# A fast-product feed-forward whose scaled operand blocks are made in another order between two stages

## The chip, the cores and the metric

The kernel runs on one core of one Trainium2 chip. The metric is the device time of one execution in microseconds (us); three executions of the kernel before gave a median of 2181.12 us. All tensors are float32. "ScalarE" is the engine ACT of the profile, "VectorE" is DVE, "GpSimd" is POOL, "TensorE" is PE.

## The reference

Two layers over a prompt of 512 tokens and 8 sample tokens (520 columns in all), width 1024:

```
x = x + 1/2 * SwiGLU_a(RMSNorm(x))
x = x + Mixer_m(RMSNorm(x))      # layer 0: gated MLP with chunked spatial mixing, layer 1: latent attention
x = x + 1/2 * SwiGLU_b(RMSNorm(x))

def swiglu(h, w_gate, w_up, w_down):
    return (silu(h @ w_gate) * (h @ w_up)) @ w_down
def rms_norm(x, g):
    return x * rsqrt(mean(x * x) + EPS) * g
```

The hidden width of a SwiGLU is 2816. There are four of them (0 to 3 here), each with its own gain and weights.

## The kernel before

**Data.** `x` is held transposed: 8 tiles of 128 channels by 520 columns. Every product is done in split precision: an operand is cut into a high part (`_hi`, a copy rounded by ScalarE) and a rest (`_lo`, value minus high part, by VectorE), and TensorE does three matmuls, high by high, rest by high, high by rest.

**Gate and up products.** In most of each SwiGLU they are done by a seven-product scheme on 2 x 2 blocks (tile pair by column half of 260). For a pair i of x tiles (2i, 2i+1) there are seven operand blocks `xw_hi[:, i, j, :]`, `xw_lo[:, i, j, :]`, j = 0 to 6. With a, b the low and high columns of the even tile and c, d those of the odd tile, all times the gain: block 0 is a, block 1 is a - b, blocks 3 and 5 are c and d, and blocks 2, 4 and 6 are differences of these, built by VectorE as `blocks[:, 2:5, :]`. `blocks[:, 0, :]` holds the gained b for this. The weights have seven block sums too (`sums_w`). A "chunk" is seven such products of 12 matmuls each (three for each of the four pairs, k = 0 to 3). Product j = 2 adds onto the PSUM bank of product 0, so ScalarE must first copy product 0 aside (L1281, `snapped`).

**The hand-over.** At the end of the stage before (gMLP output for SwiGLU 1, SwiGLU 1's last down product for SwiGLU 2, attention output for SwiGLU 3) TensorE makes eight tiles in four pairs ("down", 48 matmuls a tile). VectorE updates x (L1734, or L1874 and L1877), and in the same loop the norm operands are made: ScalarE `fast_norm` (L1307: high parts), VectorE `fast_norm` (L1839: differences and rests), ScalarE squares x and GpSimd adds the squares up (L2403), for the sum over channels that TensorE takes with a matrix of ones (`rms`, L686). ScalarE turns it into a root (L1330), VectorE into a reciprocal (L1715), which scales the products' results when they leave PSUM; so products may begin before the sum is known. In the last pair VectorE also prepares the first weight chunk (`fast_first`, L1774).

SwiGLU 0 builds the same blocks once at the start, beside products of another form, with `first_blocks` in place of `blocks`.

**Order.** There is no scheduler: each engine runs its own list in the order written, and waits on semaphores. `xg_hi_done` counts ScalarE's high parts, `xg_lo_done` VectorE's rests, `block_set` the differences, `evac_done` updates of x and evacuations of PSUM, `lo_done` weight rests. The counts at each stage's start are in class `At`.

## Time and profile before

| what | value |
|---|---|
| median of 3 runs | 2181.12 us (2179.63 to 2183.32) |
| the profiled execution, its own time | 2180.65 us |
| its span | 2178.9 us |
| PE busy | 2118.2 us, 97% |
| DVE busy | 1526.7 us, 70% |
| ACT busy | 994.8 us, 46% |
| POOL busy | 207.7 us, 10% |
| mean granted clock | 0.991 |

The profile is of one execution. Times in its rows count from the start of the span. A row of a timeline has start, duration, engine, source line, instruction, output <- inputs, partitions x elements, and in brackets the engine's idle time before it with what ended that. Consecutive instructions of VectorE and ScalarE overlap by about 0.1 us in their records.

### The profile page before, as it was taken

To read this page: it belongs to the slowest core of one execution; us is meant where nothing else is said; L and a number is where in the kernel's file an instruction comes from. 1 tells how busy PE (TensorE), PEld (TensorE's weight loads), DVE (VectorE), ACT (ScalarE), POOL (GpSimd) and SP (SyncE) were. 2 spreads that over 40 slices of the span, in tenths; PEclk is the share of its full clock that TensorE was granted. 3 is DMA by queue.
4 is the path that set the end of the run, shared out by engine and by line. 5 is a ranking of instruction groups with operands and counts; after the bars stand their busy time and mean duration, and the time that the engine had idled before them with its cause. 6 is when DMAs were issued, how large, how long until landed. Compare 5 with 4: busy or idle time off the path is not lost.

```text
span 2178.9 us, 42803 instructions
## 1 busy us (share of the span) xinstructions
PE 2118.2 (97%) x17012; PEld 2042.3 (94%) x17012; DVE 1526.7 (70%) x2222; ACT 994.8 (46%) x1549; POOL 207.7 (10%) x199
## 2 busy tenths in 40 slices
PE   8999999999998999999799999999999998999999
PEld 8999999999998999999799999987668788999999
DVE  7787685335358878597878769577665469787683
ACT  6445363433235535254444536344554445454352
POOL 0100001124031000000000000123121120000000
PEclk9999999999999999999899999999999999999999
DMA  6233233232221323232132322341221112323232
GB/s 182 78 97 116 78 98 114 80 95 74 83 79 59 102 92 116 82 112 97 59 111 92 126 78 96 116 116 36 82 88 59 59 40 78 105 89 122 74 116 76
DMA packets 203635, 198.85 MB, mean 91 GB/s; under 512 B 12071, under 2 KB 200788, under 8 KB 203252
## 3 DMA queue, kind: packets, MB, share of 16 engines
q1 hardware_dynamic: 202938, 196.67, 28.3%
q8 instruction: 86, 1.41, 0.3%
q10 hardware_dynamic: 314, 0.37, 0.1%
q14 instruction: 41, 0.34, 0.1%
q0 software_dynamic: 256, 0.07, 0.0%
HBM read 194.42 MB, written 2.66 MB: 90 GB/s over the span
## 4 chain that ended last, share of the span: by engine, by line
PE 85%; DVE 8%; ACT 3%; issue 2%; POOL 1%; DMA 0%; SPq 0%; DVEq 0%; ACTq 0%; POOLq 0%
PE main L676 35%; PE side L725 21%; PE main L725 16%; PE side L1221 2%; PE main L993 1%; DVE blocks L1859 1%; PE side L1188 1%; DVE w_lo L1710 1%; PE main L1151 1%; PE side L1024 1%; ACT w_hi L1251 1%; DVE w_lo L1737 1%; PE side L1077 1%; PE main L1056 1%; PE side L912 1%
## 5 line engine op out<-in xcount | busy, mean ns | idle before, releaser
L725 PE MATMUL side<-xw_hi,w_hi 128*128 128x260 f32 x1344 | 383.9, 286 | 25.3 <-ACT main L1281 18.0
L676 PE MATMUL main<-h_hi,w_hi 128*128 128x260 f32 x1920 | 387.5, 283 | 4.0 <-DVE x L1877 2.3
L676 PE MATMUL main<-h_hi,w_lo 128*128 128x260 f32 x1920 | 387.1, 283 | 0.0
L676 PE MATMUL main<-h_lo,w_hi 128*128 128x260 f32 x1920 | 386.4, 283 | 0.0
L725 PE MATMUL side<-xw_hi,w_lo 128*128 128x260 f32 x1344 | 381.6, 284 | 0.0
L725 PE MATMUL side<-xw_lo,w_hi 128*128 128x260 f32 x1344 | 380.2, 283 | 0.0
L676 PEld LDWEIGHTS main<-h_hi,w_hi 128*128 128x128 f32 x1920 | 296.3, 189 | 4.9 <-issue 2.7
L676 PEld LDWEIGHTS main<-h_hi,w_lo 128*128 128x128 f32 x1920 | 296.4, 189 | 0.0
L676 PEld LDWEIGHTS main<-h_lo,w_hi 128*128 128x128 f32 x1920 | 295.6, 189 | 0.0
L725 PE MATMUL main<-xw_hi,w_hi 128*128 128x260 f32 x1008 | 288.9, 287 | 2.3 <-DVE tmp_mul L1942 2.3
L725 PE MATMUL main<-xw_lo,w_hi 128*128 128x260 f32 x1008 | 288.4, 286 | 0.0
L725 PE MATMUL main<-xw_hi,w_lo 128*128 128x260 f32 x1008 | 287.9, 286 | 0.0
L725 PEld LDWEIGHTS side<-xw_hi,w_hi 128*128 128x128 f32 x1344 | 255.1, 190 | 27.5 <-ACT main L1281 19.3
L725 PEld LDWEIGHTS side<-xw_hi,w_lo 128*128 128x128 f32 x1344 | 255.1, 190 | 0.0
L725 PEld LDWEIGHTS side<-xw_lo,w_hi 128*128 128x128 f32 x1344 | 254.7, 190 | 0.1
L1710 DVE TENSOR_TENSOR w_lo<-raw,w_hi 128x2048 fp32r<-128x2048 f32 x70 | 160.5, 2293 | 108.6 <-ACT w_hi L1251 105.1
L1737 DVE TENSOR_TENSOR w_lo<-raw,w_hi 128x512 fp32r<-128x512 f32 (+1 forms) x276 | 202.6, 734 | 24.2 <-ACT w_hi L1290 13.5
L1251 ACT ACTIVATE w_hi<-raw 128x2048 fp32r<-128x2048 f32 x66 | 125.8, 1906 | 177.4 <-PE main L676 177.4
L1737 DVE TENSOR_TENSOR w_lo<-sums_w,w_hi 128x1024 fp32r<-128x1024 f32 x168 | 205.0, 1220 | 1.7 <-ACT w_hi L1273 1.6
L725 PEld LDWEIGHTS main<-xw_hi,w_hi 128*128 128x128 f32 x1008 | 192.9, 191 | 2.5 <-DVE w_lo L1737 2.5
L725 PEld LDWEIGHTS main<-xw_lo,w_hi 128*128 128x128 f32 x1008 | 192.8, 191 | 0.0
L725 PEld LDWEIGHTS main<-xw_hi,w_lo 128*128 128x128 f32 x1008 | 192.5, 191 | 0.0
(385 smaller groups left out, 3645.0 us busy)
## 6 DMA issues: line engine op xcount, KB each, us to landing
raw<-in_ffn_w_up SPq DMA_DIRECT2D x44, 1024.0 KB, 5.1
raw<-in_ffn_w_gate SPq DMA_DIRECT2D x43, 1024.0 KB, 5.1
raw<-in_ffn_w_down SPq DMA_DIRECT2D x32, 1024.0 KB, 5.2
raw<-in_gmlp_w_in SPq DMA_DIRECT2D x16, 1024.0 KB, 5.4
raw<-in_ffn_w_down SPq DMA_DIRECT2D x16, 768.0 KB, 4.4
raw<-in_gmlp_w_out SPq DMA_DIRECT2D x8, 1024.0 KB, 5.2
raw<-in_mla_w_o SPq DMA_DIRECT2D x8, 1024.0 KB, 5.5
over<-in_cache_mla SPq DMA_DIRECT2D x64, 104.0 KB, 1.9
```

The lines of the kernel that those rows point to most:

```text
L676: mm = nc.tensor.matmul(into[:, half, 0:HALF], w[:, k, m * P:(m + 1) * P], moving[:, k, half * HALF:(half + 1) * HALF], start=(k == 0 and ...
L725: mm = nc.tensor.matmul(into[j], w_tiles(w, j)[:, k, :], moving[:, k, j, :], start=(j in (0, 1) and k == 0 and i == 0), stop=(k == 3 and i ...
L912: mm = nc.tensor.matmul(side[:, bank, q * P:(q + 1) * P], v_tok[:, m, q, :], ws_t[:, g, :], start=True, stop=True)
L993: mm = nc.tensor.matmul(main[:, u % 2, half, 0:HALF], st, moving[:, k, half * HALF:(half + 1) * HALF], start=(k == 0 and i == 0), stop=(k ...
L1024: nc.tensor.matmul(side[0:w, i % 2, :], c_t[:, b * P:b * P + w], wkv[:, 4 * j:4 * j + 4, :].rearrange("p h n -> p (h n)"), start=True, sto ...
L1056: mm = nc.tensor.matmul(main[:, h % 2, half, 0:HALF], wuk_t[:, h % 2, :], qn[:, h, half * HALF:(half + 1) * HALF], start=True, stop=True)
L1077: t_ = nc.tensor.transpose(side[:, bank, i * P:(i + 1) * P], pieces[2 * (first + i // 2) + half][:, j0 + i % 2, c0:c0 + P], ident)
L1151: nc.tensor.matmul(main[:, q // 2, q % 2, 0:nk], q_rope[lo:lo + ROPE, :], kr_t[lo:lo + ROPE, 0:nk], start=False, stop=True).then_inc(score ...
L1221: mm = nc.tensor.matmul(side[:, 2, k * P:SEQ], rows[:, k, 0:KL], prob_t[:, PT_AT[k] * P:(PT_AT[k] + QB - k) * P], start=(k == 0), stop=(k ...
L1251: nc.scalar.activation(w_hi[:, 1 - s, :], raw[:, 1 - s, :], ACT.Copy).then_inc(hi_done, 1)
L1710: nc.vector.tensor_tensor(w_lo[:, 1 - s, :], raw[:, 1 - s, :], w_hi[:, 1 - s, :].bitcast(F32), ALU.subtract).then_inc(lo_done, 1)
L1737: a = nc.vector.tensor_tensor(dst, src, hi.bitcast(F32), ALU.subtract)
```

## The change

1. ScalarE's copy of the gained high columns into `blocks[:, 0, :]` moves from the odd tile's part to the even tile's part of each pair, and it signals `xg_hi_done`. So a pair has five high-part signals (six in the last), and a new counter `xh` keeps them; `xg` goes on counting rests. VectorE's first difference waits for this copy alone, and its rest of blocks 3 and 5 waits for the high parts of the odd tile.
2. In the last pair, ScalarE takes the weight step `fast_third` ahead of the odd tile's update, makes only blocks 3 and 5 there (`last_hi`), and goes on to the first chunk: copy of product 0, then high part of block 2, of blocks 4 and 6 (`last_blocks_hi`), copy of product 1, squares of tile 7, and then the weight block that stood between.
3. VectorE's `fast_first` is cut in two: two weight rests move behind the even tile's part of the last pair. In the odd part the rest of block 2 comes first, then blocks 3 and 5, then a weight rest (`rest_sums(4, 0)`), then blocks 4 and 6; the last rests are two instructions where there was one.
4. TensorE waits for the rests one product at a time (2: count 15, 3: 16, 4: 17), and takes the sum of squares ahead of product 5 instead of product 4.

```diff
-                                    x_waits = {(0, 0): x + 12, (0, 3): x + 13, (1, 3): x + 14, (2, 3): x + 16}
-                                    between = {4: rms(at, 2)}
+                                    x_waits = {(0, 0): x + 12, (0, 3): x + 13, (1, 3): x + 14, (2, 3): x + 15, (3, 3): x + 16,
+                                               (4, 3): x + 17}
+                                    between = {5: rms(at, 2)}
...
-                nc.scalar.activation(w_tiles(w_hi, 6), raw_parts(s)[:, 3], ACT.Copy).then_inc(hi_done, 1)
+                if tail:
+                    tail[0]()
+                else:
+                    nc.scalar.activation(w_tiles(w_hi, 6), raw_parts(s)[:, 3], ACT.Copy).then_inc(hi_done, 1)
                 act.wait_ge(tile_done, t + 2)
                 act.wait_ge(evac_done, e - 2)
                 nc.scalar.activation(snap[:, 0, :], main[:, 0, 0, 0:HALF], ACT.Copy, scale=-1.0).then_inc(snapped, 1)
+                if tail:
+                    tail[1]()
+                    nc.scalar.activation(w_tiles(w_hi, 6), raw_parts(s)[:, 3], ACT.Copy).then_inc(hi_done, 1)
...
                     nc.scalar.activation(xw_hi[:, i, 1, :], blocks[:, 1, :], ACT.Copy, scale=g0).then_inc(xg_hi_done, 1)
+                    nc.scalar.activation(blocks[:, 0, :], x[:, 2 * i, HALF:TOK], ACT.Copy, scale=g0).then_inc(xg_hi_done, 1)
                 elif part == 1:
-                    nc.scalar.activation(blocks[:, 0, :], x[:, 2 * i, HALF:TOK], ACT.Copy, scale=g0)
...
+            def last_hi(norm):
+
+                nc.scalar.activation(xw_hi[:, 3, 3:6:2, :], x_halves(KD - 1), ACT.Copy,
+                                     scale=gain[:, norm, KD - 1:KD]).then_inc(xg_hi_done, 1)
+
+            def last_blocks_hi(b):
+
+                act.wait_ge(block_set, b + 2)
+                nc.scalar.activation(xw_hi[:, 3, 2, :], blocks[:, 2, :], ACT.Copy).then_inc(xg_hi_done, 1)
+                act.wait_ge(block_set, b + 3)
+                nc.scalar.activation(xw_hi[:, 3, 4:7:2, :], blocks[:, 3:5, :], ACT.Copy).then_inc(xg_hi_done, 1)
...
                         if fast:
+                            if k == KD - 1:
+                                fast_third(at.tile, at.wsum)
                             act.wait_ge(evac_done, e + k + 1)
+                            if k == KD - 1:
+                                last_hi(at.norm)
+                                continue
...
+                    if between:
+                        dve.wait_ge(xg_hi_done, hi + 3)
+                        take_rest(xw_lo[:, i, 2, :], blocks[:, 2, :], xw_hi[:, i, 2, :], xg_lo_done)
+                    dve.wait_ge(xg_hi_done, hi + 2)
                     nc.vector.scalar_tensor_tensor(xw_lo[:, i, 3:6:2, :], x_halves(2 * i + 1), gains[1],
                                                    xw_hi[:, i, 3:6:2, :].bitcast(F32), ALU.mult, ALU.subtract).then_inc(xg_lo_done, 1)
                     dve.wait_ge(block_set, b + 3)
-                    dve.wait_ge(xg_hi_done, hi + 2)
-                    take_rest(xw_lo[:, i, 2:7:2, :], blocks[:, 2:5, :], xw_hi[:, i, 2:7:2, :], xg_lo_done)
+                    if between:
+                        between()
+                        dve.wait_ge(xg_hi_done, hi + 4)
+                        take_rest(xw_lo[:, i, 4:7:2, :], blocks[:, 3:5, :], xw_hi[:, i, 4:7:2, :], xg_lo_done)
+                    else:
+                        dve.wait_ge(xg_hi_done, hi + 3)
+                        take_rest(xw_lo[:, i, 2:7:2, :], blocks[:, 2:5, :], xw_hi[:, i, 2:7:2, :], xg_lo_done)
```

ScalarE in one of the pairs before the last, at the hand-over to SwiGLU 1; `blocks` is the scratch of differences, `square` the squares that GpSimd adds. Before:

```order
L1311 ACTIVATE xw_hi<-x,vectors 128x260 [waits evac_done]
L1313 ACTIVATE xw_hi<-blocks,vectors 128x260 [waits block_set]
L1257 ACTIVATE square<-x 128x520 [waits sum_done]
L1315 ACTIVATE blocks<-x,vectors 128x260 [waits evac_done]
L1316 ACTIVATE xw_hi<-x,vectors 128x2x260
L1257 ACTIVATE square<-x 128x520 [waits sum_done]
L1319 ACTIVATE xw_hi<-blocks 128x3x260 [waits block_set]
```

The same pair in the changed kernel:

```order
L1319 ACTIVATE xw_hi<-x,vectors 128x260 [waits evac_done]
L1321 ACTIVATE xw_hi<-blocks,vectors 128x260 [waits block_set]
L1322 ACTIVATE blocks<-x,vectors 128x260
L1259 ACTIVATE square<-x 128x520 [waits sum_done]
L1324 ACTIVATE xw_hi<-x,vectors 128x2x260 [waits evac_done]
L1259 ACTIVATE square<-x 128x520 [waits sum_done]
L1327 ACTIVATE xw_hi<-blocks 128x3x260 [waits block_set]
```

The copy into `blocks` stands ahead of the even tile's squares, and no longer behind the odd tile's update.

ScalarE in the last pair and the start of the first chunk; `main<-side` is the copy of product 0, `snap<-main` that of product 1. Before:

```order
L1313 ACTIVATE xw_hi<-blocks,vectors 128x260 [waits block_set]
L1257 ACTIVATE square<-x 128x520 [waits sum_done]
L1315 ACTIVATE blocks<-x,vectors 128x260 [waits evac_done]
L1316 ACTIVATE xw_hi<-x,vectors 128x2x260
L1257 ACTIVATE square<-x 128x520 [waits sum_done]
L1319 ACTIVATE xw_hi<-blocks 128x3x260 [waits block_set]
L1273 ACTIVATE w_hi<-sums_w 128x1024 [waits weights_summed,tile_done]
L1281 ACTIVATE main<-side 128x260 [waits evac_done,tile_done]
L1282 ACTIVATE w_hi<-raw 128x512
L1285 ACTIVATE snap<-main 128x260 [waits evac_done,tile_done]
```

In the changed kernel:

```order
L1321 ACTIVATE xw_hi<-blocks,vectors 128x260 [waits block_set]
L1322 ACTIVATE blocks<-x,vectors 128x260
L1259 ACTIVATE square<-x 128x520 [waits sum_done]
L1275 ACTIVATE w_hi<-sums_w 128x1024 [waits weights_summed,tile_done]
L1331 ACTIVATE xw_hi<-x,vectors 128x2x260 [waits evac_done]
L1283 ACTIVATE main<-side 128x260 [waits evac_done,tile_done]
L1337 ACTIVATE xw_hi<-blocks 128x260 [waits block_set]
L1339 ACTIVATE xw_hi<-blocks 128x2x260 [waits block_set]
L1290 ACTIVATE snap<-main 128x260 [waits evac_done,tile_done]
L1259 ACTIVATE square<-x 128x520 [waits sum_done]
L1293 ACTIVATE w_hi<-raw 128x512
```

The copy of product 0 now has one 2 x 260 instruction between it and the update of tile 7 (`evac_done`), and the last squares come six instructions after that update.

VectorE in the last pair, `w_lo` being weight rests and `x<-main,x` the updates of tiles 6 and 7. Before:

```order
L1737 TENSOR_TENSOR w_lo<-sums_w,w_hi 128x1024 [waits hi_done]
L1737 TENSOR_TENSOR w_lo<-raw,w_hi 128x512 [waits hi_done]
L1734 SCALAR_TENSOR_TENSOR x<-main,x 128x520 [waits tile_done]
L1845 TENSOR_TENSOR blocks<-x 128x260 [waits evac_done]
L1848 SCALAR_TENSOR_TENSOR xw_lo<-x,vectors,xw_hi 128x260 [waits xg_hi_done]
L1852 SCALAR_TENSOR_TENSOR xw_lo<-blocks,vectors,xw_hi 128x260 [waits xg_hi_done,block_set]
L1734 SCALAR_TENSOR_TENSOR x<-main,x 128x520 [waits tile_done]
L1856 SCALAR_TENSOR_TENSOR blocks<-x,vectors,blocks 128x260 [waits xg_hi_done,evac_done]
L1859 SCALAR_TENSOR_TENSOR blocks<-x,gain_neg,blocks 128x260 [waits block_set]
L1862 SCALAR_TENSOR_TENSOR blocks<-x,gain_neg,blocks 128x260 [waits block_set]
L1864 SCALAR_TENSOR_TENSOR xw_lo<-x,vectors,xw_hi 128x2x260
L1737 TENSOR_TENSOR xw_lo<-blocks,xw_hi 128x3x260 [waits xg_hi_done,block_set]
```

In the changed kernel (the update of tile 6 stands ahead of the first row):

```order
L1882 SCALAR_TENSOR_TENSOR xw_lo<-blocks,vectors,xw_hi 128x260 [waits xg_hi_done,block_set]
L1765 TENSOR_TENSOR w_lo<-sums_w,w_hi 128x1024 [waits hi_done]
L1765 TENSOR_TENSOR w_lo<-raw,w_hi 128x512 [waits hi_done]
L1762 SCALAR_TENSOR_TENSOR x<-main,x 128x520 [waits tile_done]
L1886 SCALAR_TENSOR_TENSOR blocks<-x,vectors,blocks 128x260 [waits xg_hi_done,evac_done]
L1889 SCALAR_TENSOR_TENSOR blocks<-x,gain_neg,blocks 128x260 [waits block_set]
L1892 SCALAR_TENSOR_TENSOR blocks<-x,gain_neg,blocks 128x260 [waits block_set]
L1765 TENSOR_TENSOR xw_lo<-blocks,xw_hi 128x260 [waits xg_hi_done]
L1898 SCALAR_TENSOR_TENSOR xw_lo<-x,vectors,xw_hi 128x2x260 [waits xg_hi_done]
L1765 TENSOR_TENSOR w_lo<-sums_w,w_hi 128x1024 [waits hi_done,block_set]
L1765 TENSOR_TENSOR xw_lo<-blocks,xw_hi 128x2x260 [waits xg_hi_done]
```

Two weight rests moved from ahead of the update of tile 6 to ahead of that of tile 7, and the update of tile 7 has the same instructions ahead of it as before.

## Rows read from the trace of the kernel before

**Rows 1.** The page, part 4: engines' shares of the chain that ended last.
```profile
PE 85%; DVE 8%; ACT 3%; issue 2%; POOL 1%; DMA 0%; SPq 0%; DVEq 0%; ACTq 0%; POOLq 0%
```

**Rows 2.** Waits of PE: us in total, times, longest us.
```profile
PE side L725 <- ACT main L1281: 18.0, 6, 5.4
...
PE main L725 <- DVE tmp_mul L1942: 2.3, 1, 2.3
PE main L676 <- DVE x L1877: 2.3, 2, 2.0
```

**Rows 3.** Timeline of PE, hand-overs to SwiGLU 1 and 3.
```profile
694.97 0.58 PE L725 MATMUL side<-xw_hi,w_hi 128*128 128x260 f32 x1 [5.02 <-ACT main L1281]
...
710.29 0.39 PE L725 MATMUL side<-xw_hi,w_hi 128*128 128x260 f32 x1 [2.05 <-ACT main L1281]
...
1814.85 0.39 PE L725 MATMUL side<-xw_hi,w_hi 128*128 128x260 f32 x1 [3.15 <-DVE x L1734]
```

**Rows 4.** Timeline of VectorE, last pair and first chunk, hand-over to SwiGLU 1.
```profile
686.05 0.69 DVE L1734 SCALAR_TENSOR_TENSOR x<-main,x 128x520 f32<-128x520 f32 x1
...
688.25 0.69 DVE L1734 SCALAR_TENSOR_TENSOR x<-main,x 128x520 f32<-128x520 f32 x1
690.22 0.49 DVE L1856 SCALAR_TENSOR_TENSOR blocks<-x,vectors,blocks 128x260 f32<-128x260 f32 x1 [1.27 <-ACT xw_hi L1316]
690.74 1.54 DVE L1859 SCALAR_TENSOR_TENSOR blocks<-x,gain_neg,blocks 128x260 f32<-128x260 f32 x1
...
693.80 0.97 DVE L1737 TENSOR_TENSOR xw_lo<-blocks,xw_hi 128x780 fp32r<-128x780 f32 x1 [0.32 <-ACT xw_hi L1319]
...
704.30 3.39 DVE L1715 RECIPROCAL rstd_all<-root 128x520 f32<-128x520 f32 x1
```

**Rows 5.** Timeline of ScalarE, same place.
```profile
692.84 0.85 ACT L1319 ACTIVATE xw_hi<-blocks 128x780 fp32r<-128x780 f32 x1 [2.20 <-DVE blocks L1862]
...
694.55 0.37 ACT L1281 ACTIVATE main<-side 128x260 f32<-128x260 f32 x1
```

**Rows 6.** Timeline of GpSimd, same place.
```profile
688.35 1.32 POOL L2403 TENSOR_TENSOR square_sum<-square_sum,square 128x520 f32<-128x520 f32 x1 [9.82 <-ACT square L1257]
690.72 1.28 POOL L2403 TENSOR_TENSOR square_sum<-square_sum,square 128x520 f32<-128x520 f32 x1 [1.05 <-ACT square L1257]
```

**Rows 7.** Line L1859, all its instructions: ns min/median/max, first and last start us.
```profile
L1859 DVE SCALAR_TENSOR_TENSOR blocks<-x,gain_neg,blocks x12: 1540/1570/1589, 653.8 to 1816.6; 128x260 f32<-128x260 f32 x12
L1859 DVE SCALAR_TENSOR_TENSOR sums_w<-x,gain_neg,sums_w x4: 487/490/490, 35.2 to 58.6; 128x260 f32<-128x260 f32 x4
```

**Rows 8.** Timeline of GpSimd in SwiGLU 0.
```profile
65.80 2.98 POOL L2408 TENSOR_TENSOR h_lo<-tmp_h,h_hi 128x520 fp32r<-128x520 f32 x2 [42.18 <-ACT h_hi L1393]
```

**Rows 9.** Timeline of VectorE in SwiGLU 0.
```profile
34.66 0.49 DVE L1856 SCALAR_TENSOR_TENSOR sums_w<-x,vectors,sums_w 128x260 f32<-128x260 f32 x1 [0.47 <-ACT xw_hi L1316]
...
65.84 1.78 DVE L1737 TENSOR_TENSOR w_lo<-raw,w_hi 128x512 fp32r<-128x512 f32 x1
```

**Rows 10.** Timeline of VectorE, first chunk of SwiGLU 3.
```profile
1821.88 1.22 DVE L1747 TENSOR_TENSOR sums_w<-raw 128x1024 f32<-128x1024 f32 x1
...
1828.17 3.39 DVE L1715 RECIPROCAL rstd_all<-root 128x520 f32<-128x520 f32 x1
```

**Rows 11.** Timeline of VectorE, hand-over to SwiGLU 2.
```profile
1019.71 2.30 DVE L1710 TENSOR_TENSOR w_lo<-raw,w_hi 128x2048 fp32r<-128x2048 f32 x1 [0.77 <-ACT w_hi L1251]
...
1033.45 2.29 DVE L1710 TENSOR_TENSOR w_lo<-raw,w_hi 128x2048 fp32r<-128x2048 f32 x1 [0.77 <-ACT w_hi L1251]
...
1054.81 1.23 DVE L1877 SCALAR_TENSOR_TENSOR x<-tmp_mul,x 128x520 f32<-128x520 f32 x1
...
1072.11 3.39 DVE L1715 RECIPROCAL rstd_all<-root 128x520 f32<-128x520 f32 x1
```

**Rows 12.** The chain that ended last, a pair of down tiles: start us, us, what.
```profile
1765.58 11.53 PE main L676 x96
```

**Rows 13.** Busy time by stretch: us, PE, PEld, DVE, ACT, POOL busy, granted clock, DMA share, GB/s.
```profile
695.00:700.00 5.00, 5.00 (x25) 5.00 (x25) 4.54 (x6) 2.70 (x5) 0.00 (x0) 0.54 0.10 31
```

More of the change, by code:

```diff
@@ L84 @@
     FIELDS = ("chunk", "extra", "tile", "evac", "h", "mul", "act", "norm", "rms", "sums", "snap", "wsum", "rows",
-              "xg", "blocks")
+              "xg", "xh", "blocks")
     def __init__(self, **counts):
         (self.chunk, self.extra, self.tile, self.evac, self.h, self.mul, self.act, self.norm, self.rms, self.sums, self.snap,
-         self.wsum, self.rows, self.xg, self.blocks) = (counts.get(f, 0) for f in self.FIELDS)
+         self.wsum, self.rows, self.xg, self.xh, self.blocks) = (counts.get(f, 0) for f in self.FIELDS)
         self.lo = self.chunk + self.extra
     def past(self, chunk=0, extra=0, tile=0, evac=0, h=0, mul=0, act=0, norm=0, rms=0, sums=0, snap=0, wsum=0, rows=0,
-             xg=0, blocks=0):
+             xg=0, xh=0, blocks=0):
         return At(chunk=self.chunk + chunk, extra=self.extra + extra, tile=self.tile + tile, evac=self.evac + evac,
@@ L96, in past @@
                   sums=self.sums + sums, snap=self.snap + snap, wsum=self.wsum + wsum, rows=self.rows + rows,
-                  xg=self.xg + xg, blocks=self.blocks + blocks)
+                  xg=self.xg + xg, xh=self.xh + xh, blocks=self.blocks + blocks)
 def ffn_past(at, plain=0, last=False):
@@ L104, in ffn_past @@
                    evac=8 * fast + 4 * plain + 8 * groups, h=2 * pairs, act=2 * pairs, norm=1, rms=1, sums=0 if last else KD,
-                   snap=6 * fast, wsum=6 * fast, rows=2 * fast + 8 * groups, xg=16 + KD * (plain > 0), blocks=16)
+                   snap=6 * fast, wsum=6 * fast, rows=2 * fast + 8 * groups, xg=16 + KD if plain else 17,
+                   xh=20 + KD if plain else 21, blocks=16)
 def bc(ap, n):
@@ L442, in program @@
         at_ffn[1] = at_gmlp.past(chunk=gmlp_chunks, tile=2 * gmlp_chunks, evac=2 * gmlp_chunks, h=GT, mul=GT, act=2 * GT, norm=1,
-                                  rms=2, sums=GT + KD, xg=KD)
+                                  rms=2, sums=GT + KD, xg=KD, xh=KD)
         at_ffn[2] = ffn_past(at_ffn[1])
@@ L447, in program @@
         at_wo = at_uq.past(chunk=4, tile=24, evac=24)
-        at_ffn[3] = at_wo.past(chunk=8, tile=16, evac=16, h=H, norm=1, sums=KD, xg=KD)
+        at_ffn[3] = at_wo.past(chunk=8, tile=16, evac=16, h=H, norm=1, sums=KD, xg=KD, xh=KD)
         P_AT = [0, 1, 3, 6]
@@ L1274, in fast_third, with fast_chunk @@
                                      ACT.Copy).then_inc(hi_done, 1)
-            def fast_chunk(s, raw_ready, t, e, w, after, middle=None):
+            def fast_chunk(s, raw_ready, t, e, w, after, middle=None, tail=None):
                 act.wait_ge(tile_done, t + 1)
@@ L1357, in gate_up @@
                         fast_chunk(0, 16 * (n // 2 + i + 1), t + 14 * i, e + 8 * i, w + 6 * i, "fast",
-                                   (lambda: rms_root(at, 2)) if first else None)
+                                   (lambda: rms_root(at, 2)) if first else None,
+                                   (lambda: last_blocks_hi(at.blocks + 13),
+                                    lambda: squares(x[:, KD - 1:KD, :], 1, at.sums - 1)) if first else None)
                         for m in range(2):
@@ L1397, in ffn @@
                     else:
-                        fast_third(t, w)
+                        if g > 0:
+                            fast_third(t, w)
                         if g == 0:
@@ L1772, in rest_sums, with fast_first @@
                 take_rest(w_block(w_lo, j, 2), sums_w[:, at:at + 2, :].rearrange("p a c -> p (a c)"), w_block(w_hi, j, 2), lo_done)
-            def fast_first(s, raw_ready, l, w):
-                sums_outer(s, raw_ready)
-                sums_second(s, w)
-                rest_raw(s, 0, 0, l + 1)
-                sums_last(s, w)
-                rest_sums(1, 2, l + 2)
-                rest_raw(s, 3, 2, l + 3)
+            def fast_first(s, raw_ready, l, w, parts=(0, 1)):
+                if 0 in parts:
+                    sums_outer(s, raw_ready)
+                    sums_second(s, w)
+                    rest_raw(s, 0, 0, l + 1)
+                    sums_last(s, w)
+                if 1 in parts:
+                    rest_sums(1, 2, l + 2)
+                    rest_raw(s, 3, 2, l + 3)
             def fast_chunk(s, raw_ready, t, e, l, w, sn, into, by, after, ready=None, late=None):
@@ L1837, in h_rest, with fast_norm @@
                                         ALU.subtract).then_inc(h_lo_done, n)
-            def fast_norm(norm, i, part, b, hi, blocks=blocks):
+            def fast_norm(norm, i, part, b, hi, blocks=blocks, between=None):
                 gains = [gain[:, norm, 2 * i + m:2 * i + m + 1] for m in range(2)]
@@ L1935, in norm_pair @@
                             for part in range(2):
-                                fast_norm(0, i, part, 4 * i + part, KD + 4 * i + 2 * part, first_blocks)
+                                fast_norm(0, i, part, 4 * i + part, KD + 5 * i + 2 * part, first_blocks)
                         def plain_up(i, m, dst):
```

12 lines of the change are left out of this document (8 added, 4 removed).

## The prediction

> **What bounds the kernel now.** I read the chain of waits first: TensorE is 85% of it, VectorE 8%, ScalarE 3% [rows 1]. So nearly all the time is matmul work that this change leaves alone, and what can be won is where the chain leaves TensorE. The waits of PE say where: 18.0 us in six waits of seven-product matmuls for ScalarE's L1281, the copy of product 0 aside [rows 2]. The timeline splits them: at each hand-over to SwiGLU 1, 2 and 3 there is one before product 2 and one before product 2 of the second half of the chunk, as 5.02 and 2.05 us at the first; at the third TensorE waits 3.15 us for the update of x before product 0 [rows 3]. ScalarE is not short of time there. L1281 is late because it stands behind L1319, which waited 2.20 us for VectorE's differences [rows 5]. VectorE in turn waited 1.27 us for ScalarE and 0.32 us for it again, and one difference took 1.54 us [rows 4]. The same line takes 0.49 us in SwiGLU 0 [rows 7], where GpSimd adds no squares. At the hand-over GpSimd's add started at 690.72, 0.02 us ahead of the long difference, for 1.28 us [rows 4, 6]. I read it as a lock: while GpSimd runs an add, a VectorE instruction with two SBUF inputs waits. It goes both ways: a weight rest that began with a GpSimd pair at 65.8 took 1.78 us, and the pair 2.98 us where two adds of 1.3 us would take 2.6 [rows 6, 8, 9]. The update of x, which reads PSUM, ran at 688.25 in its usual 0.69 us beside an add [rows 4, 6]. So VectorE's list is the bound of a hand-over, with 1.3 us to pay where an add meets it.
>
> **The second wait.** The reciprocal starts at 704.30 and TensorE goes on at 710.29, 5.99 us later [rows 3, 4]. Nothing in that stretch is changed. So each hand-over is worth what the start of its reciprocal moves.
>
> I call T the end of the update of tile 7, and split at it. Before, T is 688.94 (688.25 + 0.69), 1056.04 (1054.81 + 1.23) and 1814.80 (0.05 us ahead of the matmul that it releases), and the reciprocals start at 704.30, 1072.11 and 1828.17: 15.36, 16.07 and 13.37 us after T [rows 3, 4, 10, 11].
>
> **Behind T, the new order.** VectorE then has three differences (0.53 us from start to start, the 0.49 with its gap), the rest of block 2 (half as long as the others, about 0.4), the rest of blocks 3 and 5 (0.7), the weight rest (1.15) and the rest of blocks 4 and 6 (0.65): 4.4 us by the durations of rows 4 and 7 and by width. The copy of b is made early, so the 1.27 us are gone. The long difference is short, since the add of tile 6's squares is over by then. But the last squares are now the sixth of ScalarE's instructions behind T; they end about 3.0 us after T, GpSimd's add is ready during the weight rest and takes 1.3 us when that ends, and the rest of blocks 4 and 6 waits for it. Then come the sums and evacuations of the first chunk, whose start to reciprocal is 6.29 us where VectorE has no gap, as in SwiGLU 3 [rows 10]. In the other two it had gaps there, since the products came late. Sum: 4.4 + 1.3 + 6.3 = 12.0 us. That is 3.4 us off at the first hand-over and 4.1 at the second. At the third TensorE starts product 0 only at T, so L1281 can't run before about T + 1.7, and the high part of block 2 stands behind it: VectorE idles some 0.9 us, 12.9 us in all, 0.5 off.
>
> What is added there: one more VectorE and one or two more ScalarE instructions, counted above. TensorE will wait less before product 2 (L1281 now ends 0.7 us behind T), but again before product 6, for an evacuation that VectorE does about 1 us ahead of the reciprocal, while product 5 ends some 8 us after T: a new wait of 2 to 3 us, which the sum by the reciprocal contains. The later sum of squares is hidden: it is ready about 5 us after T, root and table load before T + 11.7. That is close: without VectorE's backlog it would be next.
>
> **Ahead of T.** In each earlier pair VectorE's idle 1.27 us goes. What is given back: the even squares are one instruction (about 0.4 us) later, so their add, which started 1.61 us after the update of tile 6 (686.74 to 688.35) [rows 4, 6] and lay beside the odd update, starts at 2.0 us and meets the first difference, up to 1.1 us, wherever VectorE runs without waiting for TensorE. Where the odd update waits for its tile, that add is past. The odd add moves from the second difference to the rest of blocks 3 and 5, same price, but the high parts and the weight copy of ScalarE (0.32 and 0.77 us of waits) now fit in beside it: 1.27 + 0.32 + 0.77, up to 2.4 us a pair [rows 4, 11].
> - SwiGLU 2: updates are two instructions, and VectorE's period is 13.74 us a pair (1019.71 to 1033.45) against TensorE's 11.53 [rows 11, 12]. Here every saved microsecond counts: 2.3 in the first pair, about 1.5 more in each of the next two (tile by tile against TensorE), 5.3 at the end of the third; less 1.3 for the add on the moved weight rest, plus 0.5 since tile 7's update, 1.23 us beside an add [rows 11], is 0.70 free of it: 4.5, of which I take 4.4. The waits of TensorE for L1877, 2.3 us [rows 2], go with it.
> - SwiGLU 1: without the second instruction of the updates (two of 0.73 us and the 0.53 of the add on one) the period is 11.75, 0.2 above TensorE's. So the third pair's odd update can move only 0.4, that pair's end 1.6 more; 1.3 comes back in the last pair, and T moves 0.6. Its bounds are 0 and 2.0.
> - SwiGLU 3: like 1, T moves 0.6.
>
> **SwiGLU 0.** The first difference waited 0.47 us for L1316 [rows 9]; it now waits for the copy one instruction ahead. Four pairs make 1.8 us. VectorE has no slack there: TensorE waited 2.3 us for L1942 behind these blocks [rows 2]. Bounds 0.5 (one pair) and 1.8; I take 1.8.
>
> **Sum.** SwiGLU 0: 1.8; 1: 0.6 + 3.4 = 4.0; 2: 4.4 + 4.1 = 8.5; 3: 0.6 + 0.5 = 1.1. Together 15.4 us. The profiled execution took 2180.65 us, so 2165.2; the median lies 0.5 us above it: 2165.7, say 2166.
>
> The cost that no row shows is who goes first when an add and a two-input instruction meet in the new places. I charge 1.3 us in full at five kinds of place. Its lower bound is 0 (row 688.35: an add beside an update costs nothing), its upper 1.1 to 1.3 each (1.54 or 1.78 us for 0.49 and 0.68).
>
> The Trainium skill, page "GPSIMD Engine Reference", section Key points, says that GpSimd shares its SBUF interfaces with VectorE, contending with instructions that have two SBUF inputs. By it the rests and weight sums that I move beside the adds must pay like the difference of rows 7, and the first rival below can't be; no row here shows an add beside a 260-column rest.
>
> **Rivals.**
> - *A, the adds cost nothing in their new places.* For: the add at 688.35 ran beside an update for nothing [rows 4, 6]. Against: the stretched instructions [rows 7 to 9]. Without them, T moves 1.7 us more in 1 and 3 and 2.4 in 2, and 1.3 more behind each T: 9.7 more, 2156.
> - *B, only the part behind T comes.* The adds on the first differences (1.1 us in each of three pairs) eat what the early copy gives, and the adds on the weight rest the remainder. For: in a pair where VectorE never waits, the first difference would start 3.4 us after the even update in both orders. Left: 3.4 + 4.1 + 0.5 and about 0.5 of SwiGLU 0: 8.5 us, 2172.5.
> - *C, it moves the wait and no more.* ScalarE's chain takes over: copy, high parts and squares in a row put the root behind VectorE's backlog, or the copies that TensorE needs before products 4 and 6 wait for more. T + 12 becomes T + 14 at the first two hand-overs, and nothing at the third: 1.4 + 2.1, 3.5 us off, 2177.5.
> - *D, slower: the clock.* After the 5.02 us wait TensorE ran at a granted 0.54 of its clock for 5 us [rows 13], the lower of its levels of 1.2 and 2.4 GHz, at half the pace. The new order has four waits of 0.8 to 3 us within 20 us. If the clock stays low for more than about 10 us per hand-over after the reciprocal, when TensorE is the bound again, 5 us each or 15 in all, the gain is gone; at 14 us each the time is 2187. Against it: the matmul behind the 2.05 us wait at 710.29 took 0.39 us, at full clock, where the one at 694.97 took 0.58 [rows 3], and no wait of the new order is as long as 5 us.
>
> The Trainium skill, page "TensorE: Matmul & The Clock Gate", Part 1, has the array fall to half rate when idle; by it the fewer long waits speak for full clock, and D asks for many short ones to count as idle.
>
> **How the numbers follow.** Forecast 0.52, A 0.12, B 0.20, C 0.10, D 0.06. The forecast's own range is 2162 to 2170 (SwiGLU 0's bounds and one add per hand-over either way). For 8 in 10 I go to 2156 and 2176, which leaves out C, D and a part of A. A measurement here can tell about 0.2%, 4.4 us, from no change: the forecast, A and B are faster by more, C half of the time no change, and D is slower in most. Faster 0.87, same 0.09, slower 0.04.
>
> **What would show it.** The reciprocals start 12 us after the update of tile 7 (13 in SwiGLU 3); PE's wait for L1281 before product 2 at the first hand-over falls from 5.0 to about 1 us, the one after the reciprocal stays at 2 to 3, and a new one for an evacuation stands before product 6. Differences take 0.49 us in the last pair, and some rest or weight instruction 1.1 to 1.3 us more, beside an add. In SwiGLU 2 the down tiles run without a wait for L1877's successor. I am wrong if the differences still take 1.5 us and VectorE idles behind T, or if TensorE's granted clock is near 0.5 for longer than 5 us behind a reciprocal.

## The result, and the profile after

| | before | after |
|---|---|---|
| median | 2180.48 us (2179.63 to 2183.32, 4 runs) | 2165.56 us (2162.85 to 2166.58, 4 runs) |
| profiled execution, its span | 2180.65, 2178.9 us | 2166.24, 2164.5 us |
| mean granted clock | 0.991 | 0.994 |

The ratio is 0.9929, with an interval of 0.9917 to 0.9941: 13 to 18 us off, where 2166.0 us was forecast. The page of the kernel after, part 4, shares of the chain that ended last, answers to [rows 1]:

```profile
PE 90%; DVE 5%; issue 2%; ACT 1%; POOL 1%; DMA 0%; SPq 0%; DVEq 0%; POOLq 0%; ACTq 0%
```

VectorE and ScalarE together have lost 5 of their 11 points. Waits of PE (us in total, times, longest), which answer to [rows 2]:

```profile
PE side L726 <- ACT main L1283: 8.3, 6, 2.4
PE side L726 <- DVE tmp_in L1841: 7.8, 4, 2.5
...
PE side L726 <- DVE x L1762: 2.2, 1, 2.2
```

The waits for the copy of product 0 (L1283, L1281 before) fall from 18.0 to 8.3 us. The waits for the down tiles' update (L1877) and for L1942 are gone. The 7.8 us for the evacuation L1841, before product 6, are 5.3 us at the three hand-overs, which are new, and 2.5 us in SwiGLU 0, where TensorE had waited 1.1 us for the same evacuation (L1811 in the kernel before):

```profile
PE side L725 <- DVE tmp_in L1811: 1.1, 1, 1.1
```

VectorE at the hand-over to SwiGLU 1, from the moved weight rest on, answers to [rows 4]:

```profile
684.20 1.80 DVE L1765 TENSOR_TENSOR w_lo<-raw,w_hi 128x512 fp32r<-128x512 f32 x1
685.92 0.69 DVE L1762 SCALAR_TENSOR_TENSOR x<-main,x 128x520 f32<-128x520 f32 x1
686.64 0.49 DVE L1886 SCALAR_TENSOR_TENSOR blocks<-x,vectors,blocks 128x260 f32<-128x260 f32 x1
687.17 0.49 DVE L1889 SCALAR_TENSOR_TENSOR blocks<-x,gain_neg,blocks 128x260 f32<-128x260 f32 x1
...
690.30 1.80 DVE L1765 TENSOR_TENSOR xw_lo<-blocks,xw_hi 128x520 fp32r<-128x520 f32 x1
...
698.31 3.38 DVE L1743 RECIPROCAL rstd_all<-root 128x520 f32<-128x520 f32 x1
```

VectorE has no idle time left here, the differences are short, and two rests take 1.80 us where they would take 0.68. The timeline of GpSimd there answers to [rows 6]:

```profile
683.56 1.88 POOL L2446 TENSOR_TENSOR square_sum<-square_sum,square 128x520 f32<-128x520 f32 x1 [7.13 <-ACT square L1259]
689.74 1.80 POOL L2446 TENSOR_TENSOR square_sum<-square_sum,square 128x520 f32<-128x520 f32 x1 [4.29 <-ACT square L1259]
```

Each add started while the instruction ahead of a long rest still ran, took 1.80 to 1.88 us instead of 1.3, and the rest after that instruction was long. TensorE's waits there answer to [rows 3]:

```profile
687.70 0.39 PE L726 MATMUL side<-xw_hi,w_hi 128*128 128x260 f32 x1 [0.35 <-ACT main L1283]
691.12 0.36 PE L726 MATMUL side<-xw_hi,w_hi 128*128 128x260 f32 x1 [0.26 <-ACT snap L1301]
697.59 0.36 PE L726 MATMUL side<-xw_hi,w_hi 128*128 128x260 f32 x1 [2.48 <-DVE tmp_in L1841]
704.30 0.39 PE L726 MATMUL side<-xw_hi,w_hi 128*128 128x260 f32 x1 [0.62 <-ACT main L1283]
```

The wait of 5.02 us before product 2 is 0.35 us, and the last row starts 5.99 us after the reciprocal, as before.

**One table for all kernels.** A hand-over is measured from the start of tile 0's update (in SwiGLU 2 the second of its two instructions) to T, and from T to the start of the reciprocal ("tail"), in each profiled execution. What lies outside is SwiGLU 0, and code that no kernel here changes. "Short adds" are explained below, under "The lock". Each run was compared with runs of the kernel before on its own chip (medians 2180.3 to 2181.6 us); the ratios below are of those.

| kernel | median us | to SwiGLU 1: to T + tail | to SwiGLU 2 | to SwiGLU 3 | sum |
|---|---|---|---|---|---|
| before | 2180.48 | 43.04 + 15.36 | 49.44 + 16.07 | 43.43 + 13.37 | 180.7 |
| new order, old wait | 2180.48 | 44.16 + 12.93 | 49.99 + 12.93 | 44.53 + 13.96 | 178.5 |
| signal alone | 2168.93 | 41.57 + 13.17 | 44.99 + 13.56 | 41.97 + 12.34 | 167.6 |
| early copy, old order | 2166.66 | 40.95 + 14.45 | 44.33 + 12.54 | 41.36 + 14.47 | 168.1 |
| new order and signal | 2170.31 | 42.70 + 12.31 | 45.54 + 12.31 | 43.06 + 13.12 | 169.0 |
| after | 2165.56 | 42.05 + 11.70 | 44.50 + 11.70 | 42.43 + 13.41 | 165.8 |
| before, short adds | 2171.03 | 41.54 + 13.79 | 44.58 + 14.69 | 41.95 + 13.78 | 170.3 |
| after, short adds | 2159.88 | 40.67 + 10.69 | 42.17 + 10.61 | 41.06 + 11.58 | 156.8 |
| after, rests back | 2164.09 | 40.95 + 12.59 | 44.37 + 11.70 | 41.36 + 12.70 | 163.7 |
| after, last square to TensorE | 2163.82 | 42.05 + 10.59 | 44.50 + 10.77 | 42.44 + 12.61 | 163.0 |
| after, no wait at SwiGLU 3 | 2164.55 | 42.07 + 11.70 | 44.53 + 11.69 | 42.47 + 11.70 | 164.2 |
| those three together | 2162.15 | 40.94 + 11.48 | 44.35 + 10.60 | 41.37 + 11.47 | 160.2 |
| two squares to TensorE, no wait | 2160.30 | 40.94 + 10.65 | 43.41 + 10.65 | 41.34 + 10.65 | 157.6 |

The hand-overs lose 14.9 us (180.7 to 165.8). SwiGLU 0, from its first rest (33.24, now 32.56) to its first down tile (89.93, now 87.04), loses 2.2 more. That is 17.1 us where the span lost 14.4: 3.4 us were lost in code that did not change, and 0.7 won before the first rest. Of the 3.4, 1.5 are between SwiGLU 0 and the first hand-over, where the kernel after has a half-clock piece (granted clock 0.57 from 476.5 to 480.5) and the kernel before has none. Another 1.8 are between the second and the third hand-over, in the attention, where TensorE fell to half clock for a while in this execution. The same place before (first row) and after (second), with the granted clock as third number from the right:

```profile
1596.00:1618.00 22.00, 18.73 (x107) 12.50 (x104) 15.41 (x47) 13.26 (x30) 7.37 (x6) 1.00 0.22 73
```
```profile
1579.00:1602.00 23.00, 19.76 (x98) 13.49 (x95) 13.67 (x39) 12.12 (x27) 7.44 (x6) 0.85 0.21 69
```

The stretch from the second reciprocal to the third hand-over took 698.0 to 702.1 us in the 13 profiles, with such half-clock pieces at different places, and all that lies outside the hand-overs (SwiGLU 0 with it) took 1996.2 to 2003.7 us. So one profile's end tells a kernel's gain only to several us, while the same steps in two kernels agree in the table to some 0.05 us (the kernel after and the one without the wait at SwiGLU 3: 42.05 and 42.07, 44.50 and 44.53).

The medians show less than these sums. In the kernel after, the hand-overs and SwiGLU 0 won 17.1 us and the median 14.9; with short adds on it, 26.1 and 20.7; with two squares to TensorE, 24.0 and 20.0. I did not follow where the remainder goes in each kernel: the table tells where time is won, and the medians how much of it the whole kernel shows.

### The profile page after: what moved, and what is told of

Read it like the earlier page. It is cut to its first block, busy times and chain, and to the rows that moved or that the text cites. A ratio compares the mean times of both kernels' runs of the same rounds, so it can differ in the third digit from the quotient of the medians.

```text
span 2164.5 us, 42809 instructions
## 1 busy us (share of the span) xinstructions
PE 2115.6 (98%) x17012; PEld 2039.2 (94%) x17012; DVE 1526.8 (71%) x2225; ACT 995.0 (46%) x1552; POOL 212.1 (10%) x199
## 4 chain that ended last, share of the span: by engine, by line
PE 90%; DVE 5%; issue 2%; ACT 1%; POOL 1%; DMA 0%; SPq 0%; DVEq 0%; POOLq 0%; ACTq 0%
PE main L677 40%; PE side L726 21%; PE main L726 16%; PE side L1223 2%; PE main L995 1%; PE side L1190 1%; DVE w_lo L1765 1%; PE main L1153 1%; PE side L1026 1%; PE side L1079 1%; PE main L1058 1%; PE side L914 1%; PE main L1140 1%; DVE rstd_all L1743 0%; PE main L1142 0%
## 5 line engine op out<-in xcount | busy, mean ns | idle before, releaser
L1765 DVE TENSOR_TENSOR w_lo<-raw,w_hi 128x512 fp32r<-128x512 f32 (+1 forms) x276 | 204.8, 742 | 24.2 <-ACT w_hi L1298 13.5
```

What stands on the lines that cost most here:

```text
L1765: a = nc.vector.tensor_tensor(dst, src, hi.bitcast(F32), ALU.subtract)
```

## Experiments

**The three edits of the change taken apart.** First the early, signalling copy alone, on the kernel before:

```diff
                     nc.scalar.activation(xw_hi[:, i, 1, :], blocks[:, 1, :], ...).then_inc(xg_hi_done, 1)
+                    nc.scalar.activation(blocks[:, 0, :], x[:, 2 * i, HALF:TOK], ...).then_inc(xg_hi_done, 1)
                 elif part == 1:
-                    nc.scalar.activation(blocks[:, 0, :], x[:, 2 * i, HALF:TOK], ...)
```

> The kernel before with one edit alone: ScalarE makes the scaled copy of b with the even tile and signals it, VectorE's first difference waits for that; the last pair and the first chunk keep their old order. Theory (VectorE's list is the bound, the order behind T is worth its own part): VectorE's idle 1.27 us go in every pair. SwiGLU 0 about 1 us, SwiGLU 1 and 3 0.6 us each ahead of T and 1.3 us behind T at the first two hand-overs, SwiGLU 2 about 4.4 us ahead of T: 9 to 10 us in all, 2171 us; a difference or the rest of blocks 3 and 5 still takes 1.5 to 1.8 us behind T, beside the add of tile 6's squares. Rival (the adds that come one ScalarE instruction later eat what the copy gives): under 3 us, 2178 us or more, and the whole gain is in the new order of the last pair.

2166.66 us, ratio 0.994 (0.9928 to 0.9953): 13.9 us off where 9 to 10 were expected. Its tail at the hand-over to SwiGLU 1 is 14.45 us, since now both adds meet differences:

```profile
686.06 1.36 DVE L1877 SCALAR_TENSOR_TENSOR blocks<-x,vectors,blocks 128x260 f32<-128x260 f32 x1
687.46 1.51 DVE L1880 SCALAR_TENSOR_TENSOR blocks<-x,gain_neg,blocks 128x260 f32<-128x260 f32 x1
```

Then the new order with b copied late again, but signalled (the last pair likewise):

```diff
-                    nc.scalar.activation(blocks[:, 0, :], ...).then_inc(xg_hi_done, 1)
                 elif part == 1:
+                    nc.scalar.activation(blocks[:, 0, :], ...).then_inc(xg_hi_done, 1)
```

> The kernel after with the early copy undone: b is copied with the odd tile again, signalled, and VectorE's first difference waits for it; the last pair and the first chunk keep their new order. Theory: the wait of 1.27 us is back in every pair, T stands where it stood before but for the weight rest (up to 1.3 us later), and behind T the reciprocal comes 2 to 3 us earlier than before at the first two hand-overs: 4 to 6 us off the kernel before, 2175 us. Rival (the early copy gives nothing): as the kernel after, 2166 us.

2170.31 us, ratio 0.9953 (0.994 to 0.9966): 5 us faster than I expected "the order" to be. The trace showed why this was no clean undoing: the first difference waits 0.65 us, not 1.27. Before, it waited for ScalarE's instruction behind the copy; the signal frees it at the copy. So I took the signal away too:

```diff
                 else:
-                    dve.wait_ge(xg_hi_done, hi + 1)
+                    dve.wait_ge(xg_hi_done, hi + 2)
                     nc.vector.scalar_tensor_tensor(blocks[:, 3, :], ...
```

> The new order of the last pair and the first chunk, and nothing else: b is copied with the odd tile, and the first difference waits, as in the kernel before, for ScalarE's next instruction behind that copy too (the high part of blocks 3 and 5). The run with the copy alone signalled waited 0.65 us there in place of 1.27. Theory: the signal is worth 0.6 us in every pair: behind each T, in three pairs of SwiGLU 2 and in SwiGLU 0's four: 5 to 6 us slower than that run, 2175 to 2176 us, which leaves 5 us for the order alone. Rival: the adds fall on other instructions and eat the difference, 2171 us.

2180.48 us, ratio 1.0 (0.9991 to 1.0009, 11 runs): the order alone is worth nothing that the median can show, though the hand-overs take 2.2 us less. Both numbers of mine were too low. What it wins in the tails (2.4 and 3.1 us) it loses in part ahead of T (1.1, 0.6 and 1.1 us, the add on the moved weight rest) and at SwiGLU 3. And at the other end of the ladder, the signal with nothing else:

```diff
-                    nc.scalar.activation(blocks[:, 0, :], x[:, 2 * i, HALF:TOK], ACT.Copy, scale=g0)
+                    nc.scalar.activation(blocks[:, 0, :], x[:, 2 * i, HALF:TOK], ACT.Copy, scale=g0).then_inc(xg_hi_done, 1)
```

> The kernel before with a signal alone: ScalarE copies b with the odd tile, as before, but signals it, and VectorE's first difference waits for that copy and not for the instruction behind it; order as before. The run with the new order and this signal took 2170.3 us, the one with the new order and the old wait 2180.5, so 10 us hang on a signal that shortens a wait by 0.62 us. Theory: 0.62 us earlier, the differences get past GpSimd's add, which then lands on the rest of blocks 3 and 5, and beside that rest ScalarE makes the two copies for which VectorE waited 0.32 and 0.77 us: 1.7 us a pair in SwiGLU 2 as long as VectorE is the bound there (about 4 us at T), 1 us behind each T and in SwiGLU 0: 8 to 9 us off the kernel before, 2172 us. Rival (the signal is worth its 0.62 us a pair and its 10 us come only together with the order): 2176 us or more.

2168.93 us, ratio 0.9949 (0.9936 to 0.9963): some 11 of the 15 us. Beyond the signal the other edits are worth little. Copying b early as well leaves the hand-overs where they were (168.1 us against 167.6), and the order takes 2.3 us off them with the early copy, 2.2 with the old wait, and adds 1.4 to the signal alone. The medians hardly tell the four kernels that have the signal apart. A pair of SwiGLU 2's hand-over in the run with the old wait:

```profile
1039.77 0.49 DVE L1888 SCALAR_TENSOR_TENSOR blocks<-x,vectors,blocks 128x260 f32<-128x260 f32 x1 [1.27 <-ACT xw_hi L1324]
1040.30 1.57 DVE L1891 SCALAR_TENSOR_TENSOR blocks<-x,gain_neg,blocks 128x260 f32<-128x260 f32 x1
...
1042.32 0.75 DVE L1900 SCALAR_TENSOR_TENSOR xw_lo<-x,vectors,xw_hi 128x520 fp32r<-128x520 f32 x1
1043.39 0.97 DVE L1767 TENSOR_TENSOR xw_lo<-blocks,xw_hi 128x780 fp32r<-128x780 f32 x1 [0.32 <-ACT xw_hi L1327]
```

and with the signal alone, from one weight rest to the next:

```profile
1016.34 2.29 DVE L1731 TENSOR_TENSOR w_lo<-raw,w_hi 128x2048 fp32r<-128x2048 f32 x1
...
1024.11 0.49 DVE L1879 SCALAR_TENSOR_TENSOR blocks<-x,vectors,blocks 128x260 f32<-128x260 f32 x1 [0.65 <-ACT blocks L1322]
1024.64 0.49 DVE L1882 SCALAR_TENSOR_TENSOR blocks<-x,gain_neg,blocks 128x260 f32<-128x260 f32 x1
1025.17 0.49 DVE L1885 SCALAR_TENSOR_TENSOR blocks<-x,gain_neg,blocks 128x260 f32<-128x260 f32 x1
1025.57 1.82 DVE L1891 SCALAR_TENSOR_TENSOR xw_lo<-x,vectors,xw_hi 128x520 fp32r<-128x520 f32 x1
1027.32 0.96 DVE L1758 TENSOR_TENSOR xw_lo<-blocks,xw_hi 128x780 fp32r<-128x780 f32 x1
1028.39 2.29 DVE L1731 TENSOR_TENSOR w_lo<-raw,w_hi 128x2048 fp32r<-128x2048 f32 x1
```

The period is 12.05 us, against 13.74 [rows 11]. The 0.62 us put the differences ahead of the add. It costs the same 1.1 us on the next rest, but the differences are now out, so ScalarE makes the two copies beside the stalled rest, and the waits of 0.32 and 0.77 us are gone: 0.62 + 0.32 + 0.77 = 1.7 us a pair, as expected. SwiGLU 0 needs only the signal too: from first rest to first down tile it took 56.7 us before and with the old wait, and 54.5 with the early copy. (With the signal alone it took 55.9 with a piece at half clock in it, which the run with signal and order, 54.5, did not have.)

**The lock.** GpSimd's adds at the hand-overs on 8 of 520 columns (`n` is 8 there), on the kernel after and on the kernel before. What is left out are the sums of squares of the other 512 columns beyond tile 0's:

```diff
-                    nc.gpsimd.tensor_tensor(square_sum[:], square_sum[:], square[:, m, :], ALU.add)...
+                    nc.gpsimd.tensor_tensor(square_sum[:, 0:n], square_sum[:, 0:n], square[:, m, 0:n], ALU.add)...
```

> The kernel after, with GpSimd's seven adds of squares at each of the three hand-overs on 8 of their 520 columns; the sums of squares of the other columns hold tile 0's alone, so that part of the norm is left out. If an add that meets a VectorE instruction with two SBUF inputs costs its whole 1.3 us where I charged it, the time falls by up to 9.7 us, to 2156 us: all differences 0.49 us, all rests of 520 columns 0.7 us, the reciprocal 10.7 us after T. Rival (the adds lie where VectorE has slack, or ScalarE's chain is as long): under 3 us, 2163 us, with VectorE waiting for ScalarE where it waited for the add.

> The kernel before with the same short adds (the sums of squares of 512 columns left out past tile 0). Theory: the long difference of each pair falls from 1.54 to 0.49 us and the odd update from 1.23 to 0.70 us; worth 1.1 us behind each T and 1.6 us in each of three pairs of SwiGLU 2, 0.2 elsewhere: 8 to 9 us off, 2172 us. The change is then still worth 14 to 16 us (2172 against 2156), since the early copy and the order work by themselves. Rival (the change works only by moving the adds off the differences): 2166 us or less, level with the kernel after.

After: 2159.88 us, ratio 0.9904 (0.989 to 0.9918); the hand-overs take 9.0 us less where up to 9.7 were expected, with tails of 10.69 and 10.61, but the median falls by 5.7 only. Before: 2171.03 us, ratio 0.9956 (0.9943 to 0.9969); 10.4 us less, where 8 to 9 were expected. So the adds' price in the hand-overs is near what was charged, in both kernels, and the change is worth 13.5 us in the hand-overs without any lock too. The Trainium skill, page "GPSIMD Engine Reference", section Key points, names contention on shared interfaces with VectorE instructions that have two SBUF inputs; the traces agree, and add that the instruction (0.68 us) ends up at 1.80, by nearly the whole add.

**Where the lock is paid.** The moved weight rests back ahead of tile 6's update:

```diff
-                        fast_first(n % 2, 16 * (n // 2 + 3), at.lo, at.wsum, (0,))
+                        fast_first(n % 2, 16 * (n // 2 + 3), at.lo, at.wsum)
...
-                            if k == KD - 2:
-                                fast_first(n % 2, 16 * (n // 2 + 3), at.lo, at.wsum, (1,))
```

> The kernel after, with the two weight rests that it moved behind tile 6's operands put back ahead of tile 6's update. Theory: in the kernel after the second of them meets the add of tile 6's squares (1.80 us for 0.68) just ahead of tile 7's update, which puts T 1.0 us later than the early copy alone gives. At the hand-overs to SwiGLU 1 and 3, where VectorE has slack ahead of tile 6, T comes 1.0 us earlier; at SwiGLU 2's, where its list is full, the add meets another instruction and nothing changes: 2 us off, 2163.5 us. Rival: tile 6's update and squares come later by the 1.8 us of the two rests, T stays: 2165.5 us.

2164.09 us, ratio 0.9919 (0.9905 to 0.9932), not told from the kernel after. T moves by 1.1 us at the first and third hand-over, as I expected, but at the first the tail gets 0.9 longer: the add now lies on the first difference, right behind T.

```profile
685.40 0.69 DVE L1762 SCALAR_TENSOR_TENSOR x<-main,x 128x520 f32<-128x520 f32 x1
686.13 1.38 DVE L1886 SCALAR_TENSOR_TENSOR blocks<-x,vectors,blocks 128x260 f32<-128x260 f32 x1
```

At the third the first difference is long too (1.36 us), but the tail falls by 0.7: TensorE waits 1.09 us for tile 7's update instead of 2.15, its granted clock stays at 1.00 behind that, and VectorE's idle time of 1.67 us is gone. So 1.8 us stay there.

```profile
1798.91 0.39 PE L726 MATMUL side<-xw_hi,w_hi 128*128 128x260 f32 x1 [1.09 <-DVE x L1762]
```

Then the squares of tile 7 taken from GpSimd and given to TensorE (GpSimd's list is one add shorter):

```diff
                     for half in range(2):
                         mm = nc.tensor.matmul(side[:, bank + half, 0:HALF], ones, square_sum[...], start=True, stop=not last)
+                        if last:
+                            mm = nc.tensor.matmul(side[:, bank + half, 0:HALF], ones, square[:, 1, ...], start=False, stop=True)
```

> The kernel after, with the squares of tile 7 left out of GpSimd's sum: TensorE takes them with two more matmuls of the matrix of ones, behind the two that it has (four of 0.4 us in place of two). So no add is behind T. Theory: the rest of blocks 4 and 6 (1.80 us) or the weight sum (2.33 us) takes its usual 0.7 or 1.2 us, and the reciprocal comes 10.6 us after T at the first two hand-overs and 12.3 us at the third: 1.1 us off each, 2162.3 us; the 0.8 us of TensorE lie in its wait before product 6 (2.5 us). Rival: the matmuls, or ScalarE's root behind them, are late, and the reciprocal stays where it is: 2165 to 2167 us.

2163.82 us, ratio 0.9917 (0.9903 to 0.993). All three tails fall, by 1.1, 0.9 and 0.8 us, where 1.1 each was expected. The theory holds in the tails; 1.7 us in the medians is below what they can tell.

**SwiGLU 3's own wait.** TensorE waited there for all updates of x, and no longer does; on the kernel after:

```diff
-                    pe.wait_ge(evac_done, e)
+                    if g == KC:
+                        pe.wait_ge(evac_done, e)
             ffn(at_ffn[3], True)
```

> The kernel after, where TensorE no longer waits ahead of SwiGLU 3 for all eight updates of x (each product still waits for the bank and the operands that it needs). In the kernel after it waited 2.15 us there for the update of tile 7, ran product 0 at half clock, and VectorE idled 1.67 us for the high part of block 2, which stands behind the copy of product 0. Theory: with product 0 started right behind the last down tile that idle goes, and the reciprocal comes 11.7 us after T as in the other two instead of 13.4: 1.7 us off, 2163.9 us. Rival: the wait only moves to product 0's last three matmuls or to the copy of product 0, under 0.5 us off.

The tail falls from 13.41 to 11.70 us, as in the other two, and TensorE's wait before product 2 is 0.36 us. The clock shows where the loss came from: in the kernel after it fell to half 0.6 us after product 0 had begun. Behind the 2.15 us wait in the kernel after (first row) and at the same work without it (second):

```profile
1801.00:1804.00 3.00, 3.00 (x16) 3.00 (x16) 1.30 (x4) 1.25 (x4) 0.00 (x0) 0.51 0.02 5
```
```profile
1801.00:1805.00 4.00, 3.74 (x30) 3.56 (x30) 4.00 (x5) 2.99 (x7) 1.80 (x1) 1.00 0.01 2
```

The median, 2164.55 us (ratio 0.9925, 0.9911 to 0.9938), can't tell it.

**Put together.** The three edits in one kernel (their diffs stand above):

> The kernel after with three edits together: the weight rests put back ahead of tile 6's update, the squares of tile 7 taken by TensorE, and no wait for all updates ahead of SwiGLU 3. Alone they gave 1.5, 1.7 and 1.0 us. Putting the rests back moved T 1.0 us forward at the hand-over to SwiGLU 1, but the add of tile 6's squares then lay on the first difference (1.38 us for 0.49), and nothing was left. Theory (an add is paid wherever VectorE has no idle time): the reciprocal comes 11.5 us after an earlier T at the first and third, 10.7 at the second; 1.1 at each of the first two and 2.8 at the third off the kernel after, 2160.5 us. Rival: the three parts add nothing to each other, 2163 us.

2162.15 us, ratio 0.9918 (0.9903 to 0.9932): the hand-overs win 5.6 us over the kernel after, where 5.0 was expected and the three alone add up to 6.6. The median shows 3.4. And with two squares instead of one given to TensorE, without the wait at SwiGLU 3, and with the weight rests where the kernel after has them:

```diff
...
-                                              square_sum[:, half * HALF:(half + 1) * HALF], start=True, stop=True)
+                        parts = [square_sum[:, cols]] + ([square[:, 0, cols], square[:, 1, cols]] if last else [])
+                        for q, part in enumerate(parts):
+                            mm = nc.tensor.matmul(side[:, bank + half, 0:HALF], ones, part, start=q == 0, stop=q == len(parts) - 1)
```

> The kernel after without TensorE's wait for all updates ahead of SwiGLU 3, and with the squares of tiles 6 and 7 taken by TensorE (six matmuls of the matrix of ones in place of two) instead of by GpSimd's adds, so that no add is near T. Theory: the moved weight rest takes 0.68 us for 1.79, T comes 1.0 us earlier at the hand-overs to SwiGLU 1 and 3 and at SwiGLU 2's, and the reciprocal comes 10.6 us after T in all three: 2 us off at each of the first two and 3.8 at the third, 7.8 in all, 2157.8 us. Rival: the four more matmuls (1.6 us) ahead of product 5 make TensorE late, since its wait before product 6 shrinks to about 1.2 us with the adds gone: 0.5 us back at each, or, if the root behind them is late, 2161 us.

2160.30 us (2157.64 to 2162.98, 4 runs), ratio 0.9904 (0.9888 to 0.992), the fastest here with the whole computation; its interval and that of the kernel after (0.9917 to 0.9941) overlap at their ends. All three tails are 10.65 us and T comes 1.1 us earlier, 8.2 us off the hand-overs where 7.8 were expected. The median shows 5.3 of it. The rest at which the first add was paid is short again:

```profile
688.09 0.69 DVE L1772 TENSOR_TENSOR w_lo<-raw,w_hi 128x512 fp32r<-128x512 f32 x1
```

## Why the prediction was right, and where it was not

- **VectorE's list bounds each hand-over; each is worth what its reciprocal moves.** Right: from reciprocal to TensorE's next product 5.99, 5.99 and 5.98 us. The hand-overs and SwiGLU 0 won 17.1 us where my sum had 15.4, and unchanged code gave 2.7 of it back in the profiled execution, mostly to the clock. So that the median (2165.56 us) lies within 0.5 us of 2166 is in part luck.
- **Behind T, 12.0 us at the first two.** Measured 11.70 both times. 12.9 at the third was too little: 13.41. The step that failed is "VectorE idles some 0.9": it idled 1.67 us. I had put the copy of product 0 at about T + 1.7, and it ran at T + 2.5 (1802.82), because product 0 began behind a wait of 2.15 us and its matmuls were at half clock from 1801.0 on. The third hand-over's tail gave nothing (0.5 forecast).

```profile
1800.37 0.39 PE L726 MATMUL side<-xw_hi,w_hi 128*128 128x260 f32 x1 [2.15 <-DVE x L1762]
...
1802.82 0.37 ACT L1283 ACTIVATE main<-side 128x260 f32<-128x260 f32 x1 [1.75 <-PE side L726]
...
1803.55 0.43 DVE L1765 TENSOR_TENSOR xw_lo<-blocks,xw_hi 128x260 fp32r<-128x260 f32 x1 [1.67 <-ACT xw_hi L1337]
```

- **Ahead of T: 0.6, 4.4, 0.6.** Measured 0.99, 4.94 and 1.00.
- **SwiGLU 0: 1.8**, the sum of four waits. Measured 2.2; I did not follow the other 0.4.
- **1.3 us for an add in each new place.** Near in size (1.80 for 0.68, so 1.1) and right in place. Rival A is out: with short adds the hand-overs won 9.0 us, where I had worked out 9.7.
- **Rival B** had the cause turned around. It let the adds eat the early copy and left the gain to the new order. In fact the order alone is worth nothing in the median, and the signal alone some 11 us. My sum did count the copy's own 1.27 us, and the 0.32 and 0.77 behind it. But it gave the gain behind T to the order as a whole, and it did not see that half of the 1.27 us was a wait for the wrong instruction. Of that failure the time shows nothing: the parts overlap, and the total of the three was right.
- **The new waits.** Before product 6, 2.48, 1.48 and 1.33 us, forecast 2 to 3. Behind the reciprocal 2 to 3 forecast, 0.62, 2.14 and 2.16 measured. Before product 2, 0.35 us at the first, about 1 forecast; at the second 2.36 us are left of 5.44. At the first hand-over, behind the reciprocal, TensorE ran the end of product 0 and product 1 at a granted clock of 0.77 (row below), came later, and so had less to wait.

```profile
700.00:704.30 4.30, 3.68 (x24) 3.47 (x23) 4.21 (x5) 1.80 (x5) 0.00 (x0) 0.77 0.00 0
```

- **Rival D** came out the other way: with fewer long waits the mean granted clock went from 0.991 to 0.994, and in the three hand-overs from 0.94, 0.87 and 0.97 to 1.00, 0.97 and 0.97. My reading against it was weak, though. That the first matmul behind a wait takes 0.39 us says nothing of the clock: so did the one at 1800.37, and 0.6 us later the clock was at half. In the kernel after none of the half-clock pieces behind a reciprocal came near the 10 us that D needs: the longest ran from about 1063.6 to 1067.2.

## What to carry to other kernels

Look at which instruction a wait really names: where a signal is missing on the producer and the waiter takes the next one's, the price is not only that instruction, but all that then falls beside something worse. An engine lock is paid wherever the waiting engine has no idle time: moving the instruction that meets the add won 0.2 and 0.1 us at two hand-overs here, and 1.8 at the third only because a wait got shorter too. Take the work off the locking engine where TensorE has a wait anyway. Test a bundled change by each part alone: gains that share a cause don't add up, and one part may carry most of them.
